# Reordering the head stage's weight copies and the last pass's early matmuls in a two-block transformer kernel

## The chip, the cores and the metric
One core of one Trainium2 chip. The metric is the device time of one execution, in microseconds (us), as the median of several.

## What is computed
Two transformer blocks on 256 tokens of width 1024, in float32. The first block has three attention branches and a feed-forward part, the second a SwiGLU part, a mixer of two recurrences (HGRN2 with 8 heads, gated delta rule with 16 heads), and another SwiGLU part. The change touches the mixer alone. Its core, for each chunk of tokens, is

```
A = where(strict, einsum('bhntk,bhnsk->bhnts', kb, k) * Lmat, 0.0)
T = triangular_solve(eye + A, eye)                  # an inverse
u = T @ (v * beta);  w = T @ (kb * exp(gam))
v_new = u - w @ S;   o = (q * exp(gam)) @ S + qk @ v_new
...
decay = exp(where(causal, b[t] - b[s], -inf))       # HGRN2, per channel
scores = einsum('bhtk,bhsk,bhtsk->bhts', q, k, decay)
...
y = sigmoid(gate_h) * (rmsnorm(o_h) * silu(hg) @ w_branch_hgrn) + sigmoid(gate_g) * y_g
```

## The kernel before
**Weights.** All weights stream from HBM in chunks of 512 KB into a ring of three slots (`w_raw`). ScalarE (ACT) copies a chunk to `w_hi`, rounded to fp32r (`split`, L567, 128x2048), VectorE (DVE) writes the remainder to `w_lo` (`w_low`, L1012), and TensorE (PE) multiplies three times for each piece (`three`, L1735 to L1737: hi by hi, hi by lo, lo by hi). `split` of chunk c waits for the data and for `gemm_done` of chunk c - 3, whose `w_hi` slot it overwrites. `w_low` waits for `split`. SyncE loads chunk c once `w_low` of chunk c - 3 is done.

**The head stage.** The projections of the mixer are 48 chunks, six for each of 8 heads. The function `head(i, gemm, main)` is written out for each engine. It is called as `head(0, True, False)`, then in a loop for i = 1 to 7 as `head(i, True, True)`, then as `head(8, False, True)`. With `gemm` it does the six projection chunks of head i, with `main` the recurrences of head i - 1. Every engine works through its own list in the order in which the code stands, and semaphores tie the lists together. This order was written out by hand.

On PE a chunk is four quarters of 12 matmuls, quarter 0 to 23 in a pass, and between them stand the small matmuls of the recurrences. Two ladders run through quarters 0 to 12.
- The inverse, by levels l = 1 to 6: `inv_z(l)` on PE (L2196), `z_copy(l)` on ACT (L830), `inv_w(l)` on PE (L2209), `inverse(l)` on DVE (L1508), `compact(l)` on ACT (L842), and `inv_z(l + 1)`. Beside it `inv_t(l - 1)` on PE (L2219) needs `compact(l - 1)`, feeds `y_copy(l - 1)` on ACT (L856, L858), and `inv_w(l)` needs that copy.
- The decays, l = 0 to 8: `middle(l)` on DVE (L1469), `level_exp(l)` on ACT (L817, L818), `decayed(l)` on DVE (L1478, L1479), `level(l)` on PE (L2172), `scored(l)` on DVE (L1488, L1495).

In level l PE's list is `inv_z(l)`, half of quarter 2l - 2, `inv_t(l - 1)`, the other half, perhaps a `level`, `inv_w(l)`, quarter 2l - 1, perhaps a `level`. Later in the pass come `vn0`, `cross` (L2265), `vn1` (L2271) with the product `r1` on DVE (L1600) between the last two, and the sum of squares of the normalised q and k (L2277), which needs `sq_ready` from ACT (L916). That in turn needs the convolution taps on DVE (L1435, L1437) and a SiLU on ACT (L904). At the end of a pass ACT copies `hv` (L976), which needs a transpose after quarter 23.

Which `split` stands where in ACT's list: the one for chunk 5 of the pass before stands behind `level_exp(2)` of the next pass. `split_j(0)` stands behind `y_copy(2)`.

**The last pass.** Pass 8 has no projections. In their place PE does early parts of the product with `w_branch_hgrn` (chunks `yh`). A part is three matmuls, `EARLY` says which parts go at which quarter, and 28 parts (four tiles by seven heads) stand at quarters 4 to 15. The operands come from `o_hi` on ACT (L849) and `o_low` on DVE (L1012), in three steps: heads 0 to 3, 4 to 6, and 7. After the pass PE does the remaining 36 parts, once `o_low` of head 7 is done (`ohl_ready`). Head 7's output needs `hsq` (L919), `sum_squares` on PE (L2260), two steps on ACT (L928, L930) and `hgrn_out` on DVE (L1518, L1521).

Of the kernel before, what the change touches and what calls it, by code (L numbers as in the profile page):

```python
# [5 lines left out]
ALU = mybir.AluOpType  # L6
# [7 lines left out]
P = 128  # L14
# [68 lines left out]
def emit(nc, ctx, a, out):  # L83
# [468 lines left out]
    def _(act):  # L552
# [243 lines left out]
        def head(i, gemm, main):  # L796
# [47 lines left out]

            def o_hi(n, k0, k1):
                if n == 1:
                    act.wait_ge(gemm_done, FIRST["yh"])
                act.wait_ge(hfin, k1)
                nc.scalar.activation(xa_hi[:, k0:k1, :], o_h[:, k0:k1, :], ACT.Copy).then_inc(ohh_ready, 1)  # L849
# [14 lines left out]
            z_copy(1)  # L864
            y_copy(0)
            level_exp(2)
            if main and gemm:
                act_split(c0 + 5 + RING - 6)
            level_exp(3)
            compact(1)  # L870
            z_copy(2)
            y_copy(1)
            if not gemm:
                o_hi(1, 0, 4)
            level_exp(4)
            compact(2)
            z_copy(3)
            level_exp(5)
            y_copy(2)
            split_j(0)  # L880
            if not gemm:
                o_hi(2, 4, GH - 1)
            compact(3)
            level_exp(6)
            z_copy(4)
            y_copy(3)
            compact(4)
            level_exp(7)
            z_copy(5)
            y_copy(4)  # L890
            if gemm:
                split_j(1)
            else:
                act_split(c0 + 5 + RING - 6)
            z_copy(6)
# [35 lines left out]
            if not gemm:  # L931
                o_hi(3, GH - 1, GH)
            if gemm:
# [30 lines left out]
            if gemm:  # L964
                act.wait_ge(y0_ready, i + 1)
                for side in range(2):
                    ins = nc.scalar.activation(kept(ntc, side), quad(nt, side), ACT.Copy)
                ins.then_inc(ntc_ready, 1)
                act.wait_ge(t_done, i + 1)
                x0 = M[:, 4, :].rearrange("p (i e c) -> p i e c", i=TT, e=2)  # L970
                nc.scalar.activation(xi, x0, ACT.Copy).then_inc(t_ready, 1)
                for side in range(2):
                    ins = nc.scalar.activation(kept(xc, side), quad(x0, side), ACT.Copy)
                ins.then_inc(xc_ready, 1)
                act.wait_ge(hvt_done, i + 1)
                nc.scalar.activation(hv.rearrange("p i c -> p (i c)"), M[:, 1, 0:T], ACT.Copy).then_inc(hv_ready, 1)  # L976
# [28 lines left out]
    def _(dve):  # L1005
# [421 lines left out]
        def head(i, gemm, main):  # L1427
# [95 lines left out]
            def o_low(k, k0, k1):  # L1523
                dve.wait_ge(ohh_ready, k)
                low_of(xa_lo[:, k0:k1, :], o_h[:, k0:k1, :], xa_hi[:, k0:k1, :]).then_inc(ohl_ready, 1)

            decayed(1)
            scored(0)
            middle(3)
            inverse(1)  # L1530
            decayed(2)
            scored(1)
            middle(4)
            if main and gemm:
                w_low(c0 + 5 + RING - 6, i, 6)
            inverse(2)
            if not gemm:
                o_low(1, 0, 4)
            decayed(3)
            scored(2)  # L1540
            middle(5)
            if gemm:
                v.tensor_copy(cwt[:, :, 0], conv[:, :, ds(i, 1)].rearrange("p j n -> p (j n)"))
                v.tensor_copy(cwt[:, :, 1], conv[:, :, ds(i + GH, 1)].rearrange("p j n -> p (j n)"))
                v.tensor_copy(cwt[:, :, 2:4], conv[:, :, ds(i * 2 + 2 * GH, 2)])
                v.tensor_copy(gbc, gdec[:, :, ds(i * 2, 2)].unsqueeze(3).to_broadcast([P, TT, 2, P])).then_inc(gbc_ready, 1)
            raw_copy(0)
            tap(0, 0)
            decayed(4)
            inverse(3)  # L1550
            if not gemm:
                o_low(2, 4, GH - 1)
            scored(3)
            middle(6)
            tap(1, 0)
            w_low_j(0)
            decayed(5)
# [9 lines left out]
            middle(8)  # L1567
            if main:
                w_low_j(1)
            tap(0, 2)  # L1570
            decayed(7)
            scored(6)
            if not gemm:
                w_low(c0 + 5 + RING - 6, i, 6)
            tap(1, 2)
# [4 lines left out]
            tap(3, 2)  # L1580
            if not main:
                w_low_j(1)
            scored(8)
# [11 lines left out]
            if gemm:  # L1595
                v.reciprocal(hr, hr)
                settle()
            if main:
                dve.wait_ge(cross_done, i)
                v.tensor_tensor(r1, vsd[:, 1, :, :], M[:, 4, 0:2 * P].rearrange("p (e c) -> p e c", e=2), ALU.subtract  # L1600
                                ).then_inc(r1_ready, 1)
            if gemm:
                v.tensor_scalar(hf, hr, lb1[:, ds(i, 1)], lb[:, ds(i, 1)], ALU.mult, ALU.add)
                v.scalar_tensor_tensor(out=hk, in0=eh, scalar=lb1[:, ds(i, 1)], in1=hr,
                                       op0=ALU.mult, op1=ALU.mult).then_inc(qk_ready, 1)
                settle()
                v.tensor_scalar(hf, hf, 2.0 ** -63, None, ALU.max).then_inc(f_ready, 1)
            if main:
                dve.wait_ge(vn1_done, i)
                for e in range(2):  # L1610
                    ins = v.tensor_scalar(vn1[:, e, :], M[:, 3, T + P * e:T + P * e + P], bst[:, 1, e:e + 1], None, ALU.mult)
                ins.then_inc(vn1_ready, 1)
                if not gemm:
                    hgrn_out()
                    o_low(3, GH - 1, GH)
            w_low_j(2)
# [111 lines left out]
    def _(pe):  # L1728
# [397 lines left out]
        def early_yh(n):  # L2126
            parts = [(tile, k) for tile in range(4) for k in range(GH - 1)]
            if n in (4, 6):
                pe.wait_ge(ohl_ready, n // 2 - 1)
            for tile, k in parts[EARLY[n][0]:EARLY[n][1]] if n in EARLY else ():  # L2130
                yh_part(tile, k, k + 1)

        EARLY = {4: (0, 2), 5: (2, 4), 6: (4, 6), 7: (6, 8), 8: (8, 11), 9: (11, 14), 10: (14, 16), 11: (16, 18),
                 12: (18, 19), 13: (19, 21), 14: (21, 24), 15: (24, 28)}

        def head(i, gemm, main):
# [121 lines left out]
            def sum_squares():  # L2258
                pe.wait_ge(hsq_ready, i)
                mm(M[:, 1, T:2 * T], ones[:], hsq, start=True, stop=True).then_inc(hss_done, 1)  # L2260

            if main:
                pe.wait_ge(vn0_ready, i)
# [4 lines left out]
            if main:  # L2268
# [127 lines left out]
```

## Time and profile before

| | |
|---|---|
| median of 3 runs | 1481.52 us (1480.78 to 1482.76) |
| the profiled execution's own time | 1482.76 us |
| its span, first to last instruction | 1481.0 us |
| busy | PE 97%, PE weight loads 91%, DVE 68%, ACT 51% |
| mean granted clock of PE | 0.995 |

The profile shows one execution. The head stage runs from about 725 to 1200 us. Passes 1 to 7 take some 57 us each; pass 8, from 1162.2 to 1199.3 us, takes 37 us. Times of single instructions are on a scale that starts with the span. The ends of matmuls are modelled, so the distance between two starts says more than a duration.

### The profile page before, as it was taken

How to read it: one execution, taken by the hardware profiler on the slowest of the kernel's cores; microseconds unless marked ns; L12 is line 12 of the kernel's file. 1: busy time of each engine (PE TensorE's matmuls, PEld its weight loads, DVE VectorE, ACT ScalarE, POOL GpSimd, SP SyncE). 2: the span in 40 equal slices, each digit the busy share in tenths (PEclk: the TensorE clock that was granted, in tenths of full speed). 3: DMA queues.
4: the chain of work that ended last, by engine and by line, in shares of the span. 5: the costliest groups of instructions: out<-in, count | busy, mean ns of one | idle time of the engine just before them, and what ended most of it. 6: DMA issues, size and time to landing. Idle time of an engine off the chain costs nothing.

```text
span 1481.0 us, 28224 instructions
## 1 busy us (share of the span) xinstructions
PE 1437.7 (97%) x10704; PEld 1352.6 (91%) x10704; DVE 1007.9 (68%) x1561; ACT 759.0 (51%) x1105; POOL 28.9 (2%) x73
## 2 busy tenths in 40 slices
PE   8999999999999999999999999999999899999998
PEld 8999989979999799999899999999999899799997
DVE  5786667675555665454798888888988765554544
ACT  4444444654444453434476576576676553544343
POOL 6000000000000000000000000000000000000000
PEclk9999999999999999999999999999999899999999
DMA  8464454555555546656553433444433255565661
GB/s 262 144 173 132 133 140 143 173 170 199 176 193 194 175 151 192 198 170 187 146 152 106 122 98 101 119 107 107 120 98 101 85 139 191 156 198 176 193 197 60
DMA packets 304640, 224.94 MB, mean 152 GB/s; under 512 B 10418, under 2 KB 288068, under 8 KB 304580
## 3 DMA queue, kind: packets, MB, share of 16 engines
q1 hardware_dynamic: 304580, 224.09, 51.0%
q8 instruction: 44, 0.72, 0.2%
q14 instruction: 16, 0.13, 0.0%
HBM read 223.02 MB, written 1.05 MB: 151 GB/s over the span
## 4 chain that ended last, share of the span: by engine, by line
PE 76%; DVE 11%; DVEq 6%; ACT 3%; issue 3%; POOL 0%; ACTq 0%; POOLq 0%
PE G L1735 15%; PE G L1737 15%; PE G L1736 15%; DVEq L1009 5%; PE M L1740 5%; PE M L1741 5%; PE M L1742 5%; DVE w_lo L1012 4%; PE M L1735 2%; PE M L1737 2%; PE M L1736 2%; ACT w_hi L567 2%; PE M L2172 1%; ACT arena L616 1%; PE M L2196 1%
## 5 line engine op out<-in xcount | busy, mean ns | idle before, releaser
L1012 DVE TENSOR_TENSOR w_lo<-w_raw,w_hi 128x2048 fp32r<-128x2048 f32 (+1 forms) x208 | 475.2, 2286 | 242.1 <-ACT w_hi L567 239.8
L1735 PE MATMUL G<-xa_hi,w_hi 128*128 128x256 f32 x2152 | 632.2, 294 | 2.6 <-DVE xa_lo L1012 2.1
L1737 PE MATMUL G<-xa_hi,w_lo 128*128 128x256 f32 x2152 | 608.4, 283 | 0.0
L1736 PE MATMUL G<-xa_lo,w_hi 128*128 128x256 f32 x2152 | 608.3, 283 | 0.0
L567 ACT ACTIVATE w_hi<-w_raw 128x2048 fp32r<-128x2048 f32 x207 | 394.9, 1908 | 253.0 <-PE G L1737 150.8
L1735 PEld LDWEIGHTS G<-xa_hi,w_hi 128*128 128x128 f32 x2152 | 411.3, 191 | 11.1 <-issue 7.6
L1736 PEld LDWEIGHTS G<-xa_lo,w_hi 128*128 128x128 f32 x2152 | 411.5, 191 | 5.3 <-issue 4.1
L1737 PEld LDWEIGHTS G<-xa_hi,w_lo 128*128 128x128 f32 x2152 | 410.9, 191 | 0.1
L1740 PE MATMUL M<-w_hi,xb_hi 128*128 128x512 f32 x304 | 118.9, 391 | 0.9 <-DVE xb_lo L1012 0.7
L1741 PE MATMUL M<-w_lo,xb_hi 128*128 128x512 f32 x304 | 118.7, 390 | 0.0
L1742 PE MATMUL M<-w_hi,xb_lo 128*128 128x512 f32 x304 | 118.3, 389 | 0.0
L742 ACT ACTIVATE arena<-G 128x256 f32<-128x256 f32 x44 | 16.9, 384 | 139.9 <-PE G L1737 139.9
L1740 PEld LDWEIGHTS M<-w_hi,xb_hi 128*128 128x128 f32 x304 | 57.2, 188 | 12.3 <-issue 1.4
L1742 PEld LDWEIGHTS M<-w_hi,xb_lo 128*128 128x128 f32 x304 | 57.1, 188 | 12.2
L1741 PEld LDWEIGHTS M<-w_lo,xb_hi 128*128 128x128 f32 x304 | 57.2, 188 | 10.5
L1012 DVE TENSOR_TENSOR xb_lo<-arena,xb_hi 128x256 fp32r<-128x256 f32 (+2 forms) x68 | 35.3, 519 | 34.4 <-ACT xb_hi L744 21.3
L1343 DVE TENSOR_TENSOR arena<-arena,G 128x256 f32<-128x256 f32 x44 | 18.5, 421 | 55.7 <-ACT arena L742 55.7
L1437 DVE SCALAR_TENSOR_TENSOR arena<-arena 128x256 f32<-128x256 f32 x96 | 42.0, 479 | 2.2
L842 ACT ACTIVATE arena<-arena 64x128 f32<-64x128 f32 x64 | 20.3, 318 | 41.6 <-DVE arena L1508 39.7
L2172 PE MATMUL M<-arena 128*128 128x64 f32 x224 | 33.3, 272 | 4.1 <-DVE arena L1495 2.8
L2196 PE MATMUL M<-arena 128*128 128x128 f32 x160 | 27.8, 296 | 9.8 <-DVE arena L1508 9.8
L2172 PEld LDWEIGHTS M<-arena 128*128 128x128 f32 x224 | 30.9, 198 | 5.9 <-DVE arena L1495 3.1
(365 smaller groups left out, 2091.9 us busy)
## 6 DMA issues: line engine op xcount, KB each, us to landing
w_raw<-in_w_in SPq DMA_DIRECT2D x166, 512.0 KB, 4.4
w_raw<-in_ffn_w_in SPq DMA_DIRECT2D x88, 512.0 KB, 4.9
w_raw<-in_w_ff SPq DMA_DIRECT2D x64, 512.0 KB, 4.1
w_raw<-in_ffn_w_out SPq DMA_DIRECT2D x44, 512.0 KB, 4.0
w_raw<-in_w_out SPq DMA_DIRECT2D x16, 512.0 KB, 4.2
w_raw<-in_w_branch_gdn SPq DMA_DIRECT2D x16, 512.0 KB, 5.2
w_raw<-in_w_branch SPq DMA_DIRECT2D x12, 512.0 KB, 4.2
w_raw<-in_w_branch_hgrn SPq DMA_DIRECT2D x8, 512.0 KB, 3.9
```

Source lines behind the costliest of these rows:

```text
L567: nc.scalar.activation(w_hi[:, slot, :], w_raw[:, slot, :], ACT.Copy).then_inc(hi_ready, 1)
L1009: v.drain()
L1012: return v.tensor_tensor(dst, src, hi.bitcast(F32), ALU.subtract)
L1437: ins = v.scalar_tensor_tensor(out=acc[:, n, :], in0=x, scalar=w, in1=acc[:, n, :], op0=ALU.mult, op1=ALU.add)
L1735: mm(out_, w[0], x[0], start=first, stop=False)
L1736: mm(out_, w[0], x[1], start=False, stop=False)
L1737: return mm(out_, w[1], x[0], start=False, stop=last_)
L1740: mm(out_, x[0], w[0], start=first, stop=False)
L1741: mm(out_, x[0], w[1], start=False, stop=False)
L1742: return mm(out_, x[1], w[0], start=False, stop=last_)
L2172: ins = mm(packed(M[:, 0, HD * b:HD * b + HD], l - 1), left[:, blk], halved(right[:, blk], l - 1, 1), start=True, stop=True)
L2196: ins = mm(packed(M[:, 3, P * b:P * b + P], l), ntc[:, b, :, :].rearrange("p e c -> p (e c)"), halved(xi[:, b, :, :].rearrange("p e c -> p ...
```

## The change
On ACT, `split` of chunk 5 moves from behind `level_exp(2)` of the next pass to the end of its own pass, before the `hv` copy. `split_j(0)` moves up from behind `y_copy(2)` to behind `y_copy(1)`. On DVE the small copies of convolution weights and `gbc` move to the start of the pass, `w_low` of chunk 5 stays behind `middle(4)` but `inverse(2)` moves behind `decayed(3)`, `scored(2)` and `middle(5)`. `w_low_j(0)` moves up by one tap, and in pass 0 `w_low_j(1)` moves ahead of the last four taps. `r1` moves behind three products of the gates. In pass 0 PE's quarter 15 moves behind the sum of squares. In pass 8 the early parts become 21 (three tiles) at quarters 2 to 13, the operands come in two steps (heads 0 to 6, then 7) with the first step already behind `y_copy(0)` on ACT and `scored(0)` on DVE, and `sum_squares` and `hgrn_out` move up.

```diff
 # ACT, head()
             level_exp(1)
             z_copy(1)
             y_copy(0)
+            if not gemm:
+                o_hi(0, GH - 1)
             level_exp(2)
-            if main and gemm:
-                act_split(c0 + 5 + RING - 6)
             level_exp(3)
             compact(1)
             z_copy(2)
             y_copy(1)
-            if not gemm:
-                o_hi(1, 0, 4)
+            split_j(0)
             level_exp(4)
             compact(2)
             z_copy(3)
+            y_copy(2)
             level_exp(5)
-            y_copy(2)
-            split_j(0)
-            if not gemm:
-                o_hi(2, 4, GH - 1)
             compact(3)
-            level_exp(6)
             z_copy(4)
             y_copy(3)
+            level_exp(6)
             compact(4)
-            level_exp(7)
             z_copy(5)
             y_copy(4)
-            if gemm:
-                split_j(1)
-            else:
-                act_split(c0 + 5 + RING - 6)
+            split_j(1)
+            level_exp(7)
             z_copy(6)
...
                 ins.then_inc(xc_ready, 1)
+            split_j(5)
+            if gemm:
                 act.wait_ge(hvt_done, i + 1)
 # DVE, head()
+            if gemm:
+                (the four copies to cwt and gbc)
             decayed(1)
             scored(0)
+            if not gemm:
+                o_low(1, 0, GH - 1)
             middle(3)
             inverse(1)
             decayed(2)
             scored(1)
             middle(4)
-            if main and gemm:
+            if main:
                 w_low(c0 + 5 + RING - 6, i, 6)
-            inverse(2)
-            if not gemm:
-                o_low(1, 0, 4)
             decayed(3)
             scored(2)
             middle(5)
-            if gemm:
-                (the four copies to cwt and gbc)
+            inverse(2)
             raw_copy(0)
             tap(0, 0)
+            w_low_j(0)
             decayed(4)
+            scored(3)
             inverse(3)
-            if not gemm:
-                o_low(2, 4, GH - 1)
-            scored(3)
             middle(6)
             tap(1, 0)
-            w_low_j(0)
...
             middle(8)
-            if main:
-                w_low_j(1)
+            w_low_j(1)
             tap(0, 2)
             decayed(7)
             scored(6)
-            if not gemm:
-                w_low(c0 + 5 + RING - 6, i, 6)
...
-            if not main:
-                w_low_j(1)
...
-            (r1, behind cross_done)
             if gemm:
                 (hf, hk, hf)
+            if main:
+                (r1, behind cross_done)
+                if not gemm:
+                    hgrn_out()
                 (vn1)
                 if not gemm:
-                    hgrn_out()
-                    o_low(3, GH - 1, GH)
+                    o_low(2, GH - 1, GH)
 # PE
-            parts = [(tile, k) for tile in range(4) for k in range(GH - 1)]
-            if n in (4, 6):
-                pe.wait_ge(ohl_ready, n // 2 - 1)
+            parts = [(tile, k) for tile in range(3) for k in range(GH - 1)]
+            if n == 2:
+                pe.wait_ge(ohl_ready, 1)
...
-        EARLY = {4: (0, 2), 5: (2, 4), 6: (4, 6), 7: (6, 8), 8: (8, 11), 9: (11, 14), 10: (14, 16), 11: (16, 18),
-                 12: (18, 19), 13: (19, 21), 14: (21, 24), 15: (24, 28)}
+        EARLY = {2: (0, 2), 3: (2, 4), 4: (4, 6), 5: (6, 8), 6: (8, 10), 7: (10, 12), 8: (12, 14), 9: (14, 16),
+                 10: (16, 18), 11: (18, 19), 12: (19, 20), 13: (20, 21)}
...
+            if main and not gemm:
+                sum_squares()
             if main:
                 (cross, quarter 14, vn1)
-            if not main:
-                quarter(15)
             if gemm:
                 pe.wait_ge(sq_ready, i + 1)
                 (sum of squares of q and k)
-            if main:
-                quarter(15)
+            quarter(15)
+            if main and gemm:
                 sum_squares()
...
-            yh_part(tile, GH - 1 if tile < 4 else 0, GH)
+            yh_part(tile, GH - 1 if tile < 3 else 0, GH)
```

## Rows read from the trace of the kernel before

**Rows 1.** The page: busy time of each engine.
```profile
PE 1437.7 (97%) x10704; PEld 1352.6 (91%) x10704; DVE 1007.9 (68%) x1561; ACT 759.0 (51%) x1105; POOL 28.9 (2%) x73
```

**Rows 2.** The waits of PE: line and releaser, us in total, times, longest.
```profile
PE M L2196 <- DVE arena L1508: 9.8, 15, 0.9
```

**Rows 3.** Timeline of PE, pass 5: start, us, engine, line, operation, what moves.
```profile
993.31 0.61 PE L2209 MATMUL M<-arena 128*128 128x128 f32 x4
...
996.27 0.72 PE L2196 MATMUL M<-arena 128*128 128x128 f32 x4 [0.50 <-DVE arena L1508]
...
1000.79 0.62 PE L2196 MATMUL M<-arena 128*128 128x128 f32 x4
...
1001.96 0.38 PE L2219 MATMUL M<-ident,arena 128*128 128x128 f32 x2
...
1010.97 0.71 PE L2196 MATMUL M<-arena 128*128 128x128 f32 x4 [0.81 <-DVE arena L1508]
...
1027.60 0.61 PE L2271 MATMUL M<-arena 128*128 128x128 f32 x4
1028.14 1.12 PE L2277 MATMUL M<-arena,ones 128*128 128x512 f32 x2
```

**Rows 4.** Timeline of ACT, same pass.
```profile
990.97 0.39 ACT L976 ACTIVATE arena<-M 128x256 f32<-128x256 f32 x1 [0.39 <-PE M L2329]
...
992.39 0.39 ACT L856 ACTIVATE arena<-M 128x256 f32<-128x256 f32 x1
...
993.09 1.91 ACT L567 ACTIVATE w_hi<-w_raw 128x2048 fp32r<-128x2048 f32 x1
...
1000.46 0.66 ACT L842 ACTIVATE arena<-arena 64x128 f32<-64x128 f32 x2 [1.67 <-DVE arena L1508]
```

**Rows 5.** Timeline of DVE, same pass.
```profile
997.32 2.28 DVE L1012 TENSOR_TENSOR w_lo<-w_raw,w_hi 128x2048 fp32r<-128x2048 f32 x1
999.68 0.74 DVE L1508 COPY_PREDICATED arena<-lmask_t,M 128x256 f32<-128x256 int32 x1
1000.22 0.32 DVE L1478 TENSOR_TENSOR arena<-arena 128x128 f32<-128x128 f32 x1
...
1001.53 0.17 DVE L1543 COPY arena<-arena 128x4 f32 x1
...
1026.49 0.42 DVE L1600 TENSOR_TENSOR arena<-arena,M 128x256 f32<-128x256 f32 x1
...
1027.72 0.29 DVE L1607 TENSOR_SCALAR arena<-arena 128x256 f32<-128x256 f32 x1
```

**Rows 6.** Timeline of pass 0: two rows of ACT, then two of PE.
```profile
742.43 1.06 ACT L904 ACTIVATE arena<-arena 128x1024 f32<-128x1024 f32 x1 [1.01 <-DVE arena L1437]
...
745.13 0.63 ACT L916 ACTIVATE arena<-arena 128x512 f32<-128x512 f32 x1
...
745.96 1.02 PE L2277 MATMUL M<-arena,ones 128*128 128x512 f32 x2
...
760.26 0.66 PE L2323 MATMUL M<-ident,arena 128*128 128x128 f32 x4 [0.47 <-DVEq L1664]
```

**Rows 7.** Timeline of PE, pass 8.
```profile
1166.32 1.09 PE L2172 MATMUL M<-arena 128*128 128x64 f32 x4 [1.31 <-DVE arena L1488]
...
1199.25 0.39 PE L1735 MATMUL G<-xa_hi,w_hi 128*128 128x256 f32 x1 [1.67 <-DVE xa_lo L1012]
```

**Rows 8.** Windows: stretch, us, busy time of each engine, PE's granted clock, DMA share, GB/s.
```profile
517.50:520.90 3.40, 1.49 (x11) 1.07 (x11) 3.17 (x4) 2.27 (x8) 0.00 (x0) 1.00 0.00 0
520.90:524.30 3.40, 3.40 (x13) 2.37 (x12) 2.89 (x6) 3.03 (x5) 0.00 (x0) 0.50 0.00 0
...
1162.60:1166.00 3.40, 1.56 (x12) 1.21 (x11) 3.15 (x5) 1.94 (x8) 0.00 (x0) 1.00 0.07 20
1166.00:1169.40 3.40, 3.08 (x14) 2.95 (x14) 2.34 (x7) 1.86 (x7) 0.00 (x0) 0.50 1.01 283
...
1210.00:1230.00 20.00, 20.00 (x169) 20.00 (x168) 11.78 (x11) 5.75 (x3) 0.00 (x0) 1.00 0.79 213
```

More of the change, by code:

```diff
@@ L843, in compact, with o_hi @@
                 ins.then_inc(xc_ready, 1)
-            def o_hi(n, k0, k1):
-                if n == 1:
+            def o_hi(k0, k1):
+                if k0 == 0:
                     act.wait_ge(gemm_done, FIRST["yh"])
@@ L931, in head @@
             if not gemm:
-                o_hi(3, GH - 1, GH)
+                o_hi(GH - 1, GH)
             if gemm:
@@ L1525, in o_low @@
                 low_of(xa_lo[:, k0:k1, :], o_h[:, k0:k1, :], xa_hi[:, k0:k1, :]).then_inc(ohl_ready, 1)
+            if gemm:
+                v.tensor_copy(cwt[:, :, 0], conv[:, :, ds(i, 1)].rearrange("p j n -> p (j n)"))
+                v.tensor_copy(cwt[:, :, 1], conv[:, :, ds(i + GH, 1)].rearrange("p j n -> p (j n)"))
+                v.tensor_copy(cwt[:, :, 2:4], conv[:, :, ds(i * 2 + 2 * GH, 2)])
+                v.tensor_copy(gbc, gdec[:, :, ds(i * 2, 2)].unsqueeze(3).to_broadcast([P, TT, 2, P])).then_inc(gbc_ready, 1)
             decayed(1)
             scored(0)
+            if not gemm:
+                o_low(1, 0, GH - 1)
             middle(3)
@@ L1541, in head @@
             middle(5)
-            if gemm:
[L1543 to L1546, printed above, removed]
+            inverse(2)
             raw_copy(0)
             tap(0, 0)
+            w_low_j(0)
             decayed(4)
+            scored(3)
             inverse(3)
-            if not gemm:
-                o_low(2, 4, GH - 1)
-            scored(3)
             middle(6)
             tap(1, 0)
-            w_low_j(0)
             decayed(5)
@@ L1597, in head @@
                 settle()
-            if main:
[L1599 to L1602, printed above, removed]
                 v.tensor_scalar(hf, hr, lb1[:, ds(i, 1)], lb[:, ds(i, 1)], ALU.mult, ALU.add)
@@ L1608, in head @@
             if main:
+                dve.wait_ge(cross_done, i)
+                v.tensor_tensor(r1, vsd[:, 1, :, :], M[:, 4, 0:2 * P].rearrange("p (e c) -> p e c", e=2), ALU.subtract
+                                ).then_inc(r1_ready, 1)
+                if not gemm:
+                    hgrn_out()
                 dve.wait_ge(vn1_done, i)
@@ L2277, in head @@
                 mm(M[:, 2, :], ones[:], eg[:, 0:2 * T], start=True, stop=True).then_inc(ss_done, 1)
-            if main:
-                quarter(15)
+            quarter(15)
+            if main and gemm:
                 sum_squares()
@@ L2335, in _ @@
         head(GH, False, True)
-        pe.wait_ge(ohl_ready, 3)
+        pe.wait_ge(ohl_ready, 2)
         for tile in range(KT):
-            yh_part(tile, GH - 1 if tile < 4 else 0, GH)
+            yh_part(tile, GH - 1 if tile < 3 else 0, GH)
             if tile == 3:
```

## The prediction, made before the changed kernel ran
> **What bounds the kernel now.** I read the page's busy times first: PE is busy for 97% of the span, so a change that adds no PE work can give or take only PE's waits and its clock [rows 1]. This one adds none. Then I read PE's waits. The largest entry of PE's is 9.8 us in 15 pieces, `inv_z` waiting for DVE's `inverse` [rows 2]; it is about two pieces in each of passes 1 to 7. Then I laid the timelines of PE, ACT and DVE of pass 5 side by side. The pieces are 0.50 us before `inv_z(2)` and 0.81 us before `inv_z(5)` [rows 3]. In a pass of the loop PE is otherwise full, so its length is PE's work plus its waits. Every new wait in it counts seven times. Last I read the windows around the two falls of the granted clock, after 520.9 and after 1166.0 us [rows 8].
>
> **Passes 1 to 7, ACT's first move.** Before, ACT copies `hv` at 990.97, makes `y_copy(0)` at 992.39 (0.39 us), and only then the 1.91 us `split` of chunk 5 [rows 4]. PE's `inv_w(1)`, which needs `y_copy(0)`, starts at 993.31 [rows 3], so ACT has 993.31 - 992.78 = 0.5 us in hand. After, the `split` stands before `hv`. It can't start before quarter 23 has ended, since it overwrites that chunk's slot; this is about 0.2 us before `hv` starts today. It takes some 1.8 us of ACT, so `hv`, `level_exp(1)`, `z_copy(1)` and `y_copy(0)` all come 1.6 us later. PE gets to `inv_w(1)` as before and waits 1.6 - 0.5 = **1.1 us, new**. The old place of the `split` hid behind PE and DVE, so nothing comes back there. DVE's `inverse(1)` starts about 0.6 us later than before, because the four small copies (now first) take it that long, and is ready for the later `inv_z(2)`: the old 0.50 us is gone.
>
> **DVE's move.** `w_low` of chunk 5 runs at 997.32 for 2.28 us and `inverse(2)` follows at 999.68 [rows 5]. It starts 0.6 us later now, and `decayed(3)`, `scored(2)` and `middle(5)` come in between: from 1000.22 to 1001.53 these take 1.3 us [rows 5]. So `inverse(2)` starts at about 999.7 + 0.6 + 1.2 = 1001.4 and gives `inv_z(3)` its operand at the end of its 0.74 us [rows 5], at 1002.2. PE reached `inv_z(3)` at 1000.79 without waiting [rows 3], and comes 1.1 - 0.5 = 0.6 us later, at 1001.4: **0.8 us, new**.
>
> **ACT's second move.** `split_j(0)` overwrites the slot of chunk 0, whose last quarter ends just before `inv_z(3)`. Before, it stood behind `y_copy(2)`, when that quarter was long done. Now ACT stands in it from `y_copy(1)` on, may start at 1001.5, and is free at 1003.35. Behind it are queued `level_exp(4)` (0.4 us), `compact(2)`, `z_copy(3)`, `y_copy(2)`. `compact(2)` takes 0.66 us [rows 4], so `inv_t(2)` gets its operand at 1004.45. PE reaches it 1.17 us after `inv_z(3)` (1001.96 - 1000.79) [rows 3], at 1003.4: **1.1 us, new**. From there everything has slack for two levels: `w_low_j(0)` now comes before `decayed(4)`, and `inverse(4)` no longer waits behind it, so the old 0.81 us [rows 3] goes. It is what I count as given back by the move of `w_low_j(0)`.
>
> **The later part.** `r1` runs at 1026.49, ahead of three products that end with the start of L1607 at 1027.72 [rows 5]. Behind them it starts at about 1027.6 and ends at 1028.05. `vn1` on PE, at 1027.60, then waits 0.45 us; but its successor was waiting until 1028.14 for ACT [rows 3], so only 0.3 us is lost.
>
> Sum of a pass: 1.1 + 0.8 + 1.1 + 0.3 - 0.50 - 0.81 = 2.0 us. Seven passes are **14.0 us**. Bounds: none of the three big new waits and the old ones gone is 0.3 - 1.3 = -1.0, or -7 us; all new waits and nothing given back is 3.3, or +23 us.
>
> **Pass 0.** PE now does the sum of squares before quarter 15. It needs `sq_ready`, for which ACT started L916 at 745.13, behind a SiLU that had waited for the taps until 742.43 [rows 6]. `w_low_j(1)`, 2.2 us of DVE, now stands before the last four taps, so both come 2.2 us later and the operand is there at 748.1. PE used to get to this product at 745.96 with quarter 15 done [rows 6], so without it at 744.5 (12 matmuls at 20 / 169 = 0.12 us [rows 8]). It waits **3.6 us**. The 0.47 us before L2323 [rows 6] goes with it, and some 0.4 us is lost less because the work behind keeps up: **+2.7 us**. DVE's and ACT's work for the next products follows within this delay.
>
> **The clock there.** The granted clock fell to 0.50, 1.2 GHz, for 3.4 us after a stretch in which PE was busy 1.49 of 3.40 us, and fell again after one with 1.56 of 3.40 [rows 8]. A wait of 3.6 us in one piece is emptier than both. I count one fall of the same length, half of 3.4 us lost: **+1.7 us** (bounds 0 and 3.4).
>
> **Pass 8.** It starts badly before as well: PE waits 1.31 us at 1166.32 [rows 7] and the clock falls [rows 8]. After, `y_copy(0)` comes 1.6 us later, then ACT copies seven heads in one piece (7/8 of L567's 1.91, about 1.7 us), until 1167.4, and DVE's `o_low` of the same size (7/8 of 2.28, 2.0 us) holds up `middle(3)` and `inverse(1)` until 1169.7. `inv_z(2)` then starts at 1170.5, where it started at 1166.32 + 1.09 = 1167.4 [rows 7]. Then comes `w_low` of the chunk, 2.3 us ahead of `inverse(2)`. By `inv_z(3)` the ladder is 4.4 us late with four parts done. From there the levels take 3.0 to 3.4 us with two parts each, against 3 to 7 before (half clock, waits), and the 2.3 us of `w_low` late in the pass are gone. I get `vn0` 0.7 us early. `sum_squares` waits for `hsq`, which two table loads on ACT hold at about where it is today. Its move up lets `hgrn_out` end at 1195.3, so PE can go on at 1197.2, when the recurrence's last product is done, in place of 1199.25 after a wait of 1.67 us [rows 7]. That is 2.0 us early, but with 7 parts of three matmuls, 7 x 0.36 = 2.5 us, more to do: **+0.5 us**. Bounds: -5 (no fall of the clock, which cost about that in 10 us) and +4 (the lag of 4.4 us is kept).
>
> **The sum.** 14.0 + 2.7 + 1.7 + 0.5 = 18.9 us on the profiled execution's 1482.76 us (span 1481.0 and 1.8 around it): 1501.7. That execution lies 1.2 us above the median, so I forecast **1500 us**, to the nearest full one.
>
> **Rivals.** *A, the new waits are hidden and the old ones go.* The change removes both of PE's regular waits, 1.3 us in each of seven passes, and the 1.67 us in pass 8. For this speak the entries of [rows 2]. Against it speak the 0.5 us that ACT has in hand before `inv_w(1)` and the slot that `split_j(0)` must wait for. It decides if ACT's copy in front of `hv` takes less than that 0.5 us of PE's time, for instance because quarter 23 ends well before ACT gets there. Then: 1481.5 - 9.1 + 2.1 (`r1`) + 2.7 + 0.5 = 1477.7 us, or 1472 with the lower bound of pass 8.
>
> *B, the clock falls in the loop.* The two new waits of 0.8 and 1.1 us are 2.2 us apart, with short matmuls and half a quarter between them; the fall after 1166.0 followed waits of this kind, the last of 1.31 us [rows 7, 8]. But in pass 5 PE has dense quarters on both sides. If it falls once in each of seven passes for 3.4 us, each costs up to 1.7 us: 1500 + 12 = 1512 us. The Trainium skill (TensorE: Matmul & The Clock Gate, Part 4: PE-mode transpose) says that transposes don't count as busy time for the clock in the way that matmuls do. By that rule B is likelier, since `inv_t(2)` stands just there, and the time would be the 1512 us of B; no row of the loop before shows a fall, so I leave B's chance low.
>
> *C, the orders matter little.* Semaphore delays and DVE's slack absorb all but one of the new waits, which balances the old ones: 1481.5 + 2.7 + 0.5 = 1485 us, or no measurable change if pass 0 is hidden too.
>
> **How the numbers follow.** The forecast has a chance of 0.60 and its own range is 1493 to 1507: 1.2 to 2.5 us a pass, the rest about as in the sum. B has 0.17 (1507 to 1517). C has 0.10 (1480 to 1493), half of which I count as no change; this kernel's runs tell about 0.2%, 3 us, from none. A has 0.13 (1470 to 1478). So: faster 0.13, same 0.05, slower 0.82. The range of 1486 to 1513 leaves out A, the lower half of C and the edge of B.
>
> **What the profile after would show.** PE's waits have entries for `inv_w` (L2209 of before) by ACT's `y_copy(0)`, about 1.1 us, eight times; for `inv_t` by `compact`, about 1 us, seven times; and `inv_z` by `inverse` at level 3, no longer at levels 2 and 5. A pass takes 59 us in place of 57. In pass 0 the sum of squares waits 3.6 us for ACT, with a clock of 0.50 right after. In pass 8 `inv_z(2)` starts 8.3 us after `inv_z(1)`, in place of 5.2. I am wrong if a pass is not longer, which would mean that ACT's `split` at the end starts earlier or costs less than I say; or if the granted clock shows falls in the loop.

## The result: 1.5% slower, and the profile after

The changed kernel takes 1504.6 us (median of 4 runs, 1503.91 to 1505.3), beside 1482.14 us for the kernel before on the same chip: a ratio of 1.0152, with a 95% interval of 1.0135 to 1.017. Its profiled execution took 1504.93 us, its span is 1503.2 us, and its mean granted clock 0.994. Two executions that some medians below take in, one of the kernel before at 4954 us and one of h1 at 1991 us, ran in a slow state of the chip; no ratio counts them. The busy times of the profiled execution answer to [rows 1]:

```profile
PE 1442.0 (96%) x10704; PEld 1352.5 (90%) x10704; DVE 1008.0 (67%) x1560; ACT 760.2 (51%) x1104; POOL 28.0 (2%) x73
```
The same number of matmuls, and a span 22.2 us longer. PE's waits (line and releaser, us in total, times, longest) answer to [rows 2]:

```profile
PE M L2196 <- ACT arena L856: 8.9, 8, 2.4
PE M L2183 <- DVE arena L1503: 8.3, 9, 3.4
PE M L2206 <- ACT arena L842: 6.0, 7, 0.9
PE M L2260 <- DVE arena L1593: 3.9, 8, 0.5
PE M L2264 <- ACT arena L909: 3.3, 1, 3.3
```
Line numbers have moved: `inv_w` is L2196, `inv_z` L2183, `inv_t` L2206, `vn1` L2260, the sum of squares of q and k L2264, `inverse` L1503. The first four entries come about once a pass, the last is pass 0. PE's timeline shows them in pass 5; the first and the last row are `inv_z(1)` of passes 5 and 6:

```profile
1001.20 0.62 PE L2183 MATMUL M<-arena 128*128 128x128 f32 x4
...
1004.82 0.71 PE L2196 MATMUL M<-arena 128*128 128x128 f32 x4 [0.92 <-ACT arena L856]
...
1007.41 0.72 PE L2183 MATMUL M<-arena 128*128 128x128 f32 x4
...
1012.71 0.72 PE L2183 MATMUL M<-arena 128*128 128x128 f32 x4 [0.62 <-DVE arena L1503]
...
1015.03 0.44 PE L2206 MATMUL M<-ident,arena 128*128 128x128 f32 x2 [0.89 <-ACT arena L842]
...
1040.36 0.71 PE L2260 MATMUL M<-arena 128*128 128x128 f32 x4 [0.47 <-DVE arena L1593]
...
1060.58 0.62 PE L2183 MATMUL M<-arena 128*128 128x128 f32 x4
```
This pass takes 59.38 us. In the kernel before, the same two starts are 57.15 us apart:

```profile
990.77 0.62 PE L2196 MATMUL M<-arena 128*128 128x128 f32 x4
...
1047.92 0.62 PE L2196 MATMUL M<-arena 128*128 128x128 f32 x4
```
The marked waits of 0.50 and 0.81 us of [rows 3] are gone, and 0.92, 0.62, 0.89 and, at `vn1`, 0.47 us have come. ACT and DVE show where from, as [rows 4, 5] do for before; first ACT (`split` of chunk 5, `y_copy(0)`, `split_j(0)`, `compact(2)`), then DVE (the last of the four small copies, `inverse(1)`, `w_low` of chunk 5, `inverse(2)`), and last `inverse(1)` of the kernel before:

```profile
1001.18 1.92 ACT L567 ACTIVATE w_hi<-w_raw 128x2048 fp32r<-128x2048 f32 x1 [0.17 <-PE G L1724]
...
1004.38 0.38 ACT L856 ACTIVATE arena<-M 128x256 f32<-128x256 f32 x1
...
1012.13 1.92 ACT L567 ACTIVATE w_hi<-w_raw 128x2048 fp32r<-128x2048 f32 x1 [2.74 <-PE G L1724]
...
1014.35 0.63 ACT L842 ACTIVATE arena<-arena 64x128 f32<-64x128 f32 x2
```
```profile
1005.03 0.43 DVE L1526 COPY arena<-arena 128x512 f32 x1
...
1006.62 0.73 DVE L1503 COPY_PREDICATED arena<-lmask_t,M 128x256 f32<-128x256 int32 x1
...
1008.46 2.28 DVE L1007 TENSOR_TENSOR w_lo<-w_raw,w_hi 128x2048 fp32r<-128x2048 f32 x1
...
1011.94 0.72 DVE L1503 COPY_PREDICATED arena<-lmask_t,M 128x256 f32<-128x256 int32 x1
```
```profile
995.50 0.72 DVE L1508 COPY_PREDICATED arena<-lmask_t,M 128x256 f32<-128x256 int32 x1
```
Behind `inv_z(1)` of its pass, `inverse(1)` starts at 1006.62 - 1001.20 = 5.42 us in place of 995.50 - 990.77 = 4.73. ACT stands 2.74 us in front of `split_j(0)`, waiting for PE to end quarter 3, with `compact(2)` queued behind. Pass 0 and pass 8 in PE's timeline, to set beside [rows 6, 7]:

```profile
746.61 1.13 PE L2264 MATMUL M<-arena,ones 128*128 128x512 f32 x2 [3.29 <-ACT arena L909]
...
1183.09 0.68 PE L2196 MATMUL M<-arena 128*128 128x128 f32 x4 [2.42 <-ACT arena L856]
...
1187.61 1.23 PE L2183 MATMUL M<-arena 128*128 128x128 f32 x4 [3.45 <-DVE arena L1503]
...
1210.39 0.70 PE L2247 MATMUL M<-arena,ones 128*128 128x256 f32 x2 [1.09 <-ACT arena L912]
```
The windows (columns as in [rows 8]) show the clock at 0.50, 1.2 GHz, in three places: twice in pass 8, and once in a later normalisation.

```profile
1185.00:1191.70 6.70, 4.09 (x19) 4.09 (x20) 6.51 (x11) 2.49 (x9) 0.00 (x0) 0.50 0.28 73
1212.20:1219.00 6.80, 6.10 (x24) 5.45 (x25) 2.49 (x7) 1.97 (x3) 0.00 (x0) 0.51 0.00 0
1307.80:1311.20 3.40, 3.40 (x13) 2.32 (x12) 3.29 (x5) 3.32 (x4) 0.00 (x0) 0.52 0.00 0
```
The balance, by starts of the same instructions in both traces. Ahead of pass 0 the kernel after is 1.4 us early: the fall of [rows 8] after 520.9 does not come in it. From the small product with `tri` to `inv_z(1)` of pass 1 it needs 24.16 in place of 21.43 us (+2.7). The seven passes take 415.6 in place of 399.8 us (+15.8). From `inv_z(1)` of pass 8 to head 8's sum of squares of g it is 42.2 in place of 38.6 us (+3.6), and 1.4 us come behind it, where the fall of the clock at 1307.8 lies (3.4 us at about half). Together: -1.4 + 2.7 + 15.8 + 3.6 + 1.4 = 22.1 us.

### The profile page after: what moved, and what is told of

Read it like the earlier page. It is cut to its first block, busy times and chain, and to the rows that moved or that the text cites. A ratio compares the mean times of both kernels' runs of the same rounds, so it can differ in the third digit from the quotient of the medians.

```text
span 1503.2 us, 28215 instructions
## 1 busy us (share of the span) xinstructions
PE 1442.0 (96%) x10704; PEld 1352.5 (90%) x10704; DVE 1008.0 (67%) x1560; ACT 760.2 (51%) x1104; POOL 28.0 (2%) x73
## 4 chain that ended last, share of the span: by engine, by line
PE 74%; DVE 12%; DVEq 5%; ACT 5%; issue 3%; POOL 0%; ACTq 0%; POOLq 0%
PE G L1722 14%; PE G L1724 14%; PE G L1723 14%; PE M L1727 5%; PE M L1728 5%; PE M L1729 5%; DVEq L1004 5%; DVE w_lo L1007 2%; PE M L1722 2%; PE M L1724 2%; PE M L1723 2%; ACT w_hi L567 2%; PE M L2196 1%; PE M L2159 1%; PE M L2183 1%
## 5 line engine op out<-in xcount | busy, mean ns | idle before, releaser
L1503 DVE COPY_PREDICATED arena<-lmask_t,M 128x256 f32<-128x256 int32 x40 | 24.4, 610 | 22.2 <-PE M L2196 22.2
L1722 PE MATMUL G<-xb_hi,w_hi 128*128 128x256 f32 x128 | 36.2, 283 | 0.0
L1724 PE MATMUL G<-xb_hi,w_lo 128*128 128x256 f32 x128 | 36.2, 283 | 0.0
L1723 PE MATMUL G<-xb_lo,w_hi 128*128 128x256 f32 x128 | 36.2, 283 | 0.0
```

The costliest lines, as they stand in the source:

```text
L1503: v.copy_predicated(halved4(xi, l, 0), halved(lmask_t[:, l, :].bitcast(I32), l, 0).unsqueeze(1).to_broadcast(shape), packed(M[:, 4, 0:T], ...
L1722: mm(out_, w[0], x[0], start=first, stop=False)
L1723: mm(out_, w[0], x[1], start=False, stop=False)
L1724: return mm(out_, w[1], x[0], start=False, stop=last_)
```

## The experiments

"A pass" is the mean over passes 2 to 7, by the starts of `inv_z(1)`; "pass 0" and "pass 8" are the two stretches of the balance. All in us; the kernel before took 1481.2 to 1482.1 us beside these runs.

| run | time | a pass | pass 0 | pass 8 |
|---|---|---|---|---|
| before | 1482.14 | 57.15 | 21.43 | 38.60 |
| after | 1504.6 | 59.40 | 24.16 | 42.22 |
| e1_split5_back | 1500.32 | 59.40 | 24.17 | 38.37 |
| e2_split0_back | 1501.77 | 58.98 | 25.72 | 39.75 |
| e3_inverse2_back | 1506.99 | 59.41 | 25.81 | 42.40 |
| e4_r1_back | 1500.06 | 58.86 | 24.17 | 39.75 |
| e5_loop_orders_back | 1491.47 | 57.68 | 25.78 | 39.67 |
| f1_split5_alone | 1486.32 | 57.60 | 21.41 | 38.87 |
| f2_split0_alone | 1491.97 | 58.23 | 21.40 | 38.61 |
| f3_inverse2_alone | 1489.3 | 58.04 | 21.42 | 39.91 |
| g1_q15_and_spread | 1502.56 | 59.40 | 24.31 | 39.64 |
| g2_wlow1_and_late_heads | 1499.39 | 59.40 | 21.99 | 38.92 |
| h1_before_inverse_first | 1481.28 | 57.04 | 21.40 | 38.54 |
| h2_before_scored_first | 1476.21 | 56.36 | 21.43 | 38.24 |

The times of before and after are medians of four executions, of h1 of ten and of h2 of five; the e, f and g rows are one execution each. The three right columns are of the profiled execution. In e1 and e5 pass 8 does the split of chunk 5 itself. Times of one kernel scatter by up to 3.1 us (h1); the length of a pass repeats to 0.06 us from pass 2 on. The verdicts on the loop go by it, and not by the whole times, which also hold what the clock and pass 8 did: e1's 1500.32 us lies below the 1502 to 1505 that its theory asked for and near the rival's 1498, but its pass 8 alone is 3.85 us shorter, and e3's 1506.99 lies above its 1503 to 1505 by the 1.6 us of a fall of the clock in pass 0.

**One part undone: the split of chunk 5 (e1).**
```diff
             level_exp(2)
+            if main:
+                act_split(c0 + 5 + RING - 6)
...
-            split_j(5)
```


> From the kernel after, only the split of chunk 5 goes back behind level_exp(2) of the next pass (in pass 8 too). A pass takes 59.38 us after the change and 57.15 before. Theory 1, the waits cover each other: PE's wait of 0.92 us at inv_w(1) goes, but the four small copies still delay DVE's inverse(1), and inverse(2) and split_j(0) are ready no sooner, so PE only gets to them earlier and waits longer: 59.0 to 59.4 us a pass, 1502 to 1505 us. Rival, each wait has its own price: 59.38 - 0.92 = 58.5 us a pass, 1498 us.

A pass is exactly as long as after. The 0.92 us at `inv_w(1)` is gone from PE's timeline, and two others stand in its place, then the old ones:

```profile
1006.86 0.66 PE L2160 MATMUL M<-arena 128*128 128x64 f32 x4 [0.48 <-DVE arena L1484]
...
1008.02 0.72 PE L2184 MATMUL M<-arena 128*128 128x128 f32 x4 [0.50 <-DVE arena L1504]
...
1013.31 0.72 PE L2184 MATMUL M<-arena 128*128 128x128 f32 x4 [0.62 <-DVE arena L1504]
1015.63 0.44 PE L2207 MATMUL M<-ident,arena 128*128 128x128 f32 x2 [0.89 <-ACT arena L842]
```
`inverse(2)` stands at 1012.54, which is 10.74 us behind this pass's `inv_z(1)` at 1001.80. After, it is 1011.94 - 1001.20 = 10.74 too. `inverse(1)` stands at 5.44 us here and 5.42 after, and `inv_z(2)` at 6.22 and 6.21, though ACT's `split` is back in its old place. DVE's list, with the four small copies at its head, sets this; that PE gets there earlier gains nothing. No run moves the copies alone, but f1 has ACT's move without them: `inverse(1)` at 4.72 us and `inv_z(2)` at 6.00.

**One part undone: split_j(0) and w_low_j(0) (e2).**
```diff
-            split_j(0)
             level_exp(4)
...
             y_copy(2)
+            split_j(0)
...
-            w_low_j(0)
             decayed(4)
...
             tap(1, 0)
+            w_low_j(0)
```


> From the kernel after, only split_j(0) on ACT goes back behind y_copy(2) and w_low_j(0) on DVE back behind tap(1, 0). Theory 1: PE's wait of 0.89 us at inv_t(2) goes, but inverse(4) stands behind w_low_j(0) again, so the old wait of 0.8 us before inv_z(5) returns: 59.1 to 59.5 us a pass, 1503 to 1505 us. Rival: the old wait doesn't return since everything is late anyway, 59.38 - 0.89 = 58.5 us a pass, 1498 us.

A pass is 0.42 us shorter. The 0.89 us is gone, and before `inv_z(5)` a part of the old wait is back:

```profile
1023.21 0.71 PE L2183 MATMUL M<-arena 128*128 128x128 f32 x4 [0.46 <-DVE arena L1503]
```
My 59.1 to 59.5 was 0.1 too high, the rival's 58.5 was 0.5 too low: half is covered.

**One part undone: inverse(2) (e3).**
```diff
                 w_low(c0 + 5 + RING - 6, i, 6)
+            inverse(2)
...
             middle(5)
-            inverse(2)
```


> From the kernel after, only inverse(2) on DVE goes back directly behind w_low. Theory 1: PE's wait of 0.62 us before inv_z(3) goes, but split_j(0) still ends when chunk 0 is done plus 1.9 us; it starts 0.6 us earlier too, since it waits for PE's quarter 3, which lies ahead of inv_z(3). So inv_t(2) is bound by the end of quarter 3 + 1.92 (split) + 0.4 + 0.7 us, as now, and waits 1.5 us: 59.2 to 59.4 us a pass, 1503 to 1505 us. Rival: 59.38 - 0.62 = 58.8 us a pass, 1500 us.

Nothing comes back; PE's wait has moved to `inv_t(2)`, 1.78 us in place of 0.89:

```profile
1016.90 0.44 PE L2206 MATMUL M<-ident,arena 128*128 128x128 f32 x2 [1.78 <-ACT arena L842]
```
`split_j(0)` starts 1014.00 - 1003.07 = 10.93 us behind `inv_z(1)` here, and 1012.13 - 1001.20 = 10.93 us in the kernel after. It waits for PE's quarter 3, which in both follows `inverse(1)` and `inv_z(2)`.

**One part undone: r1 (e4).**
```diff
             if gemm:
                 v.reciprocal(hr, hr)
                 settle()
+            if main:
+                dve.wait_ge(cross_done, i)
+                v.tensor_tensor(r1, vsd[:, 1, :, :], M[:, 4, 0:2 * P].rearrange("p (e c) -> p e c", e=2), ALU.subtract
+                                ).then_inc(r1_ready, 1)
+            if gemm:
```


> From the kernel after, only r1 on DVE goes back ahead of the three products of the gates. Both theories: PE's wait of 0.47 us at vn1 goes. Theory 1: the products of the gates are later, the next product waits for them or for ACT, and 0.2 to 0.3 us a pass come back: 59.1 us, 1502.5 us. Rival: all 0.47 us, 58.9 us a pass, 1501 us.

The rival is right: 0.54 us a pass come back, the whole wait and a little more. What is queued behind `r1` had slack enough.

**All orders of the loop undone (e5).** ACT's and DVE's lists as before, with `r1`, pass 0 and pass 8 new.

> From the kernel after, every order of ACT and DVE in the loop that the ladders see goes back to that of the kernel before (split of chunk 5, split_j(0), w_low_j(0), inverse(2), inverse(3), the small copies, level_exp); r1, pass 0 and pass 8 keep the new order, but for the split of chunk 5, which pass 8 does itself. Theory 1, the waits cover each other: though each part alone gave back 0 to 0.4 us, all together give back 59.38 to 57.15 + 0.5 (r1) = 57.65 us a pass, 12 us, so 1492 to 1494 us. Rival: most of the loss is in something else that stays, such as the DMA queue or pass 0's state carried into the loop, and the parts give back the sum of what they gave alone: 59.38 - 0.41 = 59.0 us a pass, 1502 us.

57.68, as theory 1 had it. Undone singly the three parts gave 0, 0.42 and 0 us; undone together, with the copies and the order of `inverse(3)` and `level_exp`, they give 1.72. In the loop only `r1` is left of the change in e5, so 57.68 - 57.15 = 0.53 us is its price alone, the same as e4's.

**Each part alone, on the kernel before (f1, f2, f3).** The edits are those of the change: `split_j(5)` ahead of the `hv` copy; `split_j(0)` behind `y_copy(1)` with `w_low_j(0)` ahead of `decayed(4)`; `inverse(2)` behind `middle(5)`.

> From the kernel before, only the split of chunk 5 moves to the end of its own pass, ahead of the hv copy. Theory 1: PE waits 0.9 us at inv_w(1), and inv_z(2) comes so much later that its old 0.5 us is covered: 57.15 + 0.9 - 0.5 = 57.6 us a pass, 1485 us. Rival, the prices add: 57.15 + 0.9 = 58.1 us a pass, 1488 us.

57.60, theory 1. PE waits 0.92 us at `inv_w(1)`, and no wait is marked at `inv_z(2)`.

> From the kernel before, only split_j(0) moves up behind y_copy(1), and w_low_j(0) up ahead of decayed(4). Theory 1: ACT stands in the split from the end of quarter 3 on, and inv_t(2) waits the whole distance, 1.8 us as in the run with inverse(2) back; the old 0.81 us before inv_z(5) goes: 57.15 + 1.8 - 0.8 = 58.1 us a pass, 1489 us. Rival, its price is the 0.9 us that it shows in the kernel after: 57.15 + 0.9 - 0.8 = 57.25 us, 1482 us.

58.23, theory 1. PE waits 1.77 us at `inv_t(2)`, twice what the kernel after shows there:

```profile
1005.51 1.91 ACT L567 ACTIVATE w_hi<-w_raw 128x2048 fp32r<-128x2048 f32 x1 [2.74 <-PE G L1737]
```
```profile
1008.41 0.44 PE L2219 MATMUL M<-ident,arena 128*128 128x128 f32 x2 [1.77 <-ACT arena L842]
```
`inv_z(1)` of this pass is at 995.29, so `split_j(0)` starts 10.22 us behind it, 0.71 less than after, e1 and e3, where the small copies hold `inverse(1)` back. In all four `inv_t(2)` comes 2.90 us behind the start of `split_j(0)`.

> From the kernel before, only inverse(2) moves behind decayed(3), scored(2) and middle(5). Theory 1: it starts 1.3 us later and PE waits 0.9 us at inv_z(3), less what the old 0.8 us before inv_z(5) then gives back, since w_low_j(0) is no later than before: 57.15 + 0.1 to 0.9 = 57.3 to 58.1 us a pass, 1483 to 1489 us. Rival, the price is the 0.62 us that it shows in the kernel after: 57.8 us a pass, 1486 us.

58.04, the upper end of theory 1, though the marked wait is the rival's: PE waits 0.63 us before `inv_z(3)`, and the 0.80 us before `inv_z(5)` stays. `inv_z(3)` starts 0.78 us later than before, and what follows it 0.88. The surcharges alone are 0.45, 1.08 and 0.89 us, with `r1`'s 0.54 (as undone in e4) together 2.96; the change itself costs 2.25 a pass. In f2's pass 1 the clock fell, after this product and in this stretch (the clock is the 0.58):

```profile
773.94 0.44 PE L2219 MATMUL M<-ident,arena 128*128 128x128 f32 x2 [1.77 <-ACT arena L842]
```
```profile
775.00:778.40 3.40, 3.40 (x20) 3.38 (x20) 3.07 (x8) 1.43 (x6) 0.00 (x0) 0.58 0.27 59
```
That pass took 59.54 us. In the other six of f2, and in all seven of e3 with the same wait, it did not fall.

**Pass 0 and pass 8 (g1, g2).**
g1 is:
```diff
+            if not main:
+                quarter(15)
...
-        EARLY = {..., 8: (12, 14), 9: (14, 16), 10: (16, 18), 11: (18, 19), 12: (19, 20), 13: (20, 21)}
+        EARLY = {..., 8: (12, 14), 9: (14, 15), ..., 14: (19, 20), 15: (20, 21)}
```
g2 has `o_hi` of heads 0 to 6 behind `y_copy(1)`, `o_low` behind `inverse(2)`, the 21 early parts at quarters 4 to 13, and:
```diff
+            if main:
+                w_low_j(1)
             tap(0, 2)
...
             tap(3, 2)
+            if not main:
+                w_low_j(1)
```


> From the kernel after, two edits that lie 400 us apart. In pass 0, PE's quarter 15 goes back ahead of the sum of squares: PE's wait there, 3.29 us, loses the 1.4 us of the quarter and is about 1.9 us, so pass 0 costs 1.4 us less if nothing behind it is bound by another engine, and nothing less if the work behind (ACT's and DVE's, from that sum on) sets the pace. In pass 8, the same 21 early parts are spread over quarters 2 to 15 (one each from quarter 9 on), so that PE has work between its last three waits. Theory 1: the second fall of the clock, 6.8 us from 1212.2 on, does not come and 3.4 us are back, less what the waits take in their new place: from inv_z(1) to the sum of squares of head 8, 39 to 40 us in place of 42.2. Rival: the parts take no wait's place, because hsq and hgrn_out on ACT and DVE set the end, and the fall stays: 42 us. In all 1500 us by theory 1 and 1503 us by the rival.

In pass 0 PE's wait fell to 1.87 us, yet the stretch is no shorter (24.31 us), and now the clock falls (0.68 in the second window):

```profile
746.00:750.00 4.00, 2.13 (x10) 1.46 (x9) 2.49 (x5) 3.92 (x5) 0.00 (x0) 0.90 0.11 27
750.00:754.00 4.00, 4.00 (x26) 4.00 (x26) 3.77 (x10) 3.61 (x5) 0.00 (x0) 0.68 0.10 14
```
Less the 1.6 us that such a fall costs here (e3 against after), the 24.31 us would be about 1.4 less than after, as theory 1 asks; that is an estimate, and the rival, another engine setting the pace, isn't excluded. In pass 8 there is no second fall, and 39.64 us is what theory 1 asked for. But it proves nothing: e2 and e4, with pass 8 as after, show 39.75 us and no second fall either. The theory that the spread early parts keep the clock up stays open.

> From the kernel after, two edits far apart. In pass 0, w_low_j(1) on DVE goes back behind the last four taps, and PE's order stays: the 2.2 us of w_low are what made the operand late, so the wait of 3.29 us falls to 1.1 us, and pass 0 costs 2.2 us less. In pass 8, o_hi of heads 0 to 6 goes back behind y_copy(1), o_low behind inverse(2), and the early parts (still 21) stand at quarters 4 to 13 as in the kernel before. Theory 1, the early copies make the pass late: PE's 3.45 us before inv_z(2) falls by DVE's 2.0 us of o_low, and from inv_z(1) to the sum of squares of head 8 it takes 40 us in place of 42.2. Rival, the end of the pass is set by the clock and by the last waits, which stay: 42 us. In all 1500.4 us by theory 1 and 1502.4 us by the rival.

Pass 0: the wait is 1.13 us, 21.99 us in place of 24.16, as theory 1 has it. `w_low_j(1)` on DVE is the cause. Pass 8: 38.92 us, against 39.75 us of like executions (without the second fall): the early place of the seven heads' copies and of the products that use them costs 0.8 us, not 2. The price holds what the clock did: in g2 it is at 0.50 for some 10 us here, as long as in the kernel before, and for some 7 us in after.

**A new order from the kernel before (h1, h2).** It aims at PE's own waits in a pass. h1 moves, on DVE, `inverse(1)` ahead of `middle(3)`, `inverse(2)` ahead of `middle(4)`, `inverse(4)` ahead of `tap(2, 0)`, `decayed(7)` and `scored(6)` ahead of `tap(0, 2)`, and on ACT `compact(1)` and `compact(2)` ahead of `level_exp(3)` and `level_exp(4)`. h2 moves besides `decayed(8)` and `scored(7)` ahead of `tap(2, 2)`, and:
```diff
             inverse(4)
-            tap(2, 0)
             decayed(6)
+            scored(5)
             middle(7)
+            tap(2, 0)
             tap(3, 0)
-            scored(5)
```


> A new order, from the kernel before, that aims at PE's own waits in a pass: on DVE inverse(1) ahead of middle(3), inverse(2) ahead of middle(4), inverse(4) ahead of tap(2, 0), decayed(7) and scored(6) ahead of tap(0, 2); on ACT compact(1) ahead of level_exp(3) and compact(2) ahead of level_exp(4). Nothing else moves. Theory 1, PE bounds a pass but for its waits of 0.50, 0.81 and 0.23 us, and each of these comes from one instruction that stands one place too late: 57.15 - 1.5 = 55.6 us a pass and 1471 us. Rival, the waits cover others, as they did in the kernel after, and half comes back: 56.4 us a pass, 1476 us.

Both were wrong: 57.04 us a pass and a ratio of 0.9996 (0.9985 to 1.0006). The 0.81 us before `inv_z(5)` is gone, and PE stands one level on:

```profile
1012.74 0.66 PE L2172 MATMUL M<-arena 128*128 128x64 f32 x4 [0.71 <-DVE arena L1495]
```


> From the kernel before, the seven moves of the run before this one, and two more on DVE: decayed(6), scored(5) and middle(7) now stand ahead of tap(2, 0) and tap(3, 0), and decayed(8) and scored(7) ahead of tap(2, 2). In the run before this one PE's 0.81 us before inv_z(5) was gone, but 0.71 us stood before level 6, for scored(5), which was queued behind the two taps (1.8 us of DVE), and 0.19 us before level 8 for scored(7). Theory 1: what set the pace there was DVE's queue, and with scored(5) ahead of the taps both waits go: 57.03 - 0.71 - 0.19 = 56.1 us a pass, 1475 us. Rival: DVE has too much to do between w_low_j(0) and inverse(5), and the wait only moves on to inv_w(5) or to level 7, as it did once: 56.9 to 57.0 us a pass, 1480.5 us.

56.36 us a pass, 1476.21 us against 1481.15, a ratio of 0.9965 (0.9951 to 0.9978). Theory 1 is right in kind; of its 0.9 us a pass, 0.7 came. Of PE's waits marked in pass 5 these are left:

```profile
993.52 0.72 PE L2196 MATMUL M<-arena 128*128 128x128 f32 x4 [0.35 <-DVE arena L1508]
...
1020.34 0.49 PE L2253 MATMUL M<-arena 128*128 128x128 f32 x2 [0.22 <-DVE arena L1491]
```
So a version 0.35% faster than the kernel before is had from it by moves of the same kind; h1's seven alone gave nothing clear of the scatter.

## Why the prediction was right, step by step

It said 1500 us and slower, and 1504.6 was measured; its sum for the profiled execution was 1501.7, and 1504.93 was measured. The direction and the main term, PE's new waits in the loop, are shown by the traces and by e5. That the whole came within 3.3 us is partly luck: the loop was 1.8 us more than said and pass 8 3.1 us more, and the 1.7 us for the clock in pass 0 did not come. (Ahead of the head stage and behind it, 1.4 us went and 1.4 us came, by the clock too.)

- **ACT's first move**: 1.1 us forecast, 0.92 shown, and `inv_z(2)`'s marked 0.50 gone, as said. f1 gives its price alone, 0.45 us; in the kernel after it is nothing (e1).
- **The four small copies**: the text let them delay `inverse(1)` by 0.6 us without a cost. The rows show 0.69 us, and that this, not ACT's `split`, sets the start of `inv_z(2)` in the kernel after, 0.71 us later than before. It is the step that the prediction had wrong.
- **DVE's move**: 0.8 forecast, 0.62 shown, and nothing when undone (e3). **ACT's second move**: 1.1 forecast, 0.89 shown. The old 0.81 us went. Where `w_low_j(0)` stays (f1, f3) it stays too, 0.81 and 0.80; where that moves with `split_j(0)` (f2, after) it is gone, and with both back in e2 0.46 of it returns. No run moves `w_low_j(0)` alone.
- **The later part**: 0.3 forecast, 0.54 measured by e4. I took the product behind `vn1` to be waiting anyway; that credit was wrong.
- **The sum of a pass**: 2.0 forecast, 2.25 measured, 14.0 against 15.8 us. The marked waits of pass 5 explain less: 0.92 + 0.62 + 0.89 + 0.47 - 0.50 - 0.81 = 1.6 us. The starts of the same instructions, counted from `inv_z(1)`, place the rest:

| pass 5, us behind `inv_z(1)` | before | after | later by |
|---|---|---|---|
| `inv_w(1)` | 2.54 | 3.62 | 1.08 |
| `inv_z(2)` | 5.50 | 6.21 | 0.71 |
| `inv_z(3)` | 10.02 | 11.51 | 1.49 |
| `inv_t(2)` | 11.19 | 13.83 | 2.64 |
| `inv_z(4)` | 14.82 | 17.53 | 2.71 |
| `inv_z(5)` | 20.20 | 21.94 | 1.74 |
| `vn0` | 32.40 | 34.10 | 1.70 |
| `vn1` | 36.83 | 39.16 | 2.33 |
| next `inv_z(1)` | 57.15 | 59.38 | 2.23 |

  Each wait that PE has pushes its product back by about 0.16 us more than the profile marks: 1.08 for 0.92, 0.78 for 0.62, 0.63 for 0.47, and in f2 1.93 for 1.77; the 0.81 us that went gave 0.97. A group of `inv_z` or `inv_w` that PE waited for also takes longer itself, 0.71 to 0.72 us in place of 0.61 to 0.62, and what follows is later by this 0.1. `inv_z(2)` of after has this 0.72 with no wait marked. My 2.0 was near because the waits were forecast 0.2 too high each, and what is not marked made up for it; that is luck.
- What the text called terms of a sum are waits that follow each other, but not prices. Undone alone, ACT's first move (e1) and `inverse(2)` (e3) give back nothing. At `inv_t(2)` only the latest counts: that is the 0.71 us from the small copies, then quarter 3, then `split_j(0)` and `compact(2)`, at 13.83 us in after, e1 and e3. `inverse(2)` is ready 10.74 us behind `inv_z(1)`, and PE's wait for it only takes from the wait at `inv_t(2)`. The prediction's own times (DVE ready at 1002.2, ACT at 1004.45) had the last part in them.
- **Pass 0**: +2.7 forecast, +2.73 measured; a wait of 3.6 forecast, 3.29 shown. g2 confirms `w_low_j(1)` as its cause, for 2.2 us of the 2.7.
- **The clock there**: +1.7 forecast, none in the profile of after. With the same wait as in after, the fall came in e2, e3 and e5 (25.72 to 25.81 us) and did not in after, e1 and e4 (24.16, 24.17). Its price, 1.6 us, was right; that it comes at all was not to be counted on, for it came in three of six. The profile of after has an extra fall at 1307.8 us, and none at 520.9.
- **Pass 8**: +0.5 forecast, +3.6 measured, the term that was mis-sized most. `inv_z(2)` starts 8.2 us behind `inv_z(1)` (8.3 forecast). But the sum did not count a second fall of the clock, behind the last waits. It came in two of the four executions with this order (after and e3); e2 and e4 have none and show 39.75 us, +1.15. So the order costs about 1.2 us, and the second fall 2.5 us. What of the 1.2 us is the low clock isn't shown: e1, with the `split` of chunk 5 behind `level_exp(2)` again, has `inv_z(2)` at 7.1 us and only some 3.4 us at 0.50, and takes 38.37 us, no more than before; e5, with the same 7.1 us and some 7 us at 0.50, takes 39.67.
- **Rival B**, a fall in the loop, did not come in the kernel after. The text bore it up with a rule of the Trainium skill (TensorE: Matmul & The Clock Gate, Part 4: PE-mode transpose), by which transposes don't count as busy time for the clock in the way that matmuls do. The runs speak little for it here: with 1.8 us of wait right before the transposes `inv_t(2)`, one pass in fourteen saw a fall (f2, e3). **Rivals A and C** needed hidden waits; every one that was forecast is in the profile, though two of them turned out to be covered by others.

## What to carry to other kernels

When three engines with lists in fixed order meet at one point, ask for each list when it gets there by itself; what counts is the latest, and the price of a move is how far it pushes that one back. A wait that a profile shows is not what its removal gives: look one and two instructions on for who is ready just behind it, and compare the starts of the same instructions in both traces, which hold what no wait is marked for. A few short copies at the head of a list (0.7 us here) can set the pace of all that stands behind them. Where the engine that sets the pace waits for a short operation, look for long work queued in front of it that nobody needs yet (here two taps in front of `scored(5)`); that move came on top of h1's seven, which alone gave nothing clear of the scatter, and together they were worth 0.35%.

## What had not been expected of the hardware

In pass 0 a single wait of 3.3 us on PE was followed by a fall of the clock in three executions and not in three others:

```profile
746.00:750.00 4.00, 3.39 (x23) 2.91 (x24) 2.56 (x4) 3.93 (x6) 0.00 (x0) 1.00 0.00 0
```
```profile
746.00:750.00 4.00, 3.15 (x9) 2.11 (x10) 2.49 (x5) 3.58 (x5) 0.00 (x0) 0.62 0.01 2
```
The first window is of the kernel after (a wait of 3.29 us, as in e1 and e4), the second of e3 (3.32 us), whose order of pass 0 is the same. The other two with a fall, e2 and e5 (3.31 and 3.33 us), have `split_j(0)` and `w_low_j(0)` elsewhere. In g1 a wait of 1.87 us had a fall behind it. So the length of the wait alone doesn't tell; what does, these runs leave open. It is a spread of 1.6 us at this place, and of 2.5 us at the end of pass 8.

The clearest case lies ahead of the head stage, where all fourteen kernels are alike. After a stretch in which PE was busy for 1.46 to 1.51 of 3.40 us, the clock fell in eight of the profiled executions (before, e1, e4, f1, g1, g2, h1, h2) and not in six (after, e2, e3, e5, f2, f3). The kernel after, to set beside the first two windows of [rows 8]:

```profile
517.50:520.90 3.40, 1.49 (x13) 1.29 (x12) 3.24 (x5) 2.27 (x9) 0.00 (x0) 1.00 0.00 0
520.90:524.30 3.40, 3.17 (x21) 2.31 (x20) 3.11 (x6) 3.38 (x5) 0.00 (x0) 1.00 0.00 0
```
So the prediction's reason for a fall in pass 0, a wait emptier than such a stretch, is no reason to count on one.
